# Sample-token values in column strips, state updates by quarters, shifted buffers and HGRN queries on VectorE in a two-layer hybrid decoder step

## The reference, cut to what matters

```python
for li in range(DEPTH):
    h = h + 0.5 * swiglu(rms_norm(h, ffn1_norm[li]), ffn1_w_gu[li], ffn1_w_down[li])
    u = rms_norm(h, mix_norm[li])
    m, s = gla_mixer(u, ...) if li % 2 == 0 else hgrn2_mixer(u, ...)
    h = h + m
    h = h + 0.5 * swiglu(rms_norm(h, ffn2_norm[li]), ffn2_w_gu[li], ffn2_w_down[li])
    gate = jax.nn.sigmoid(rms_norm(h, ple_norm[li]) @ ple_w_gate[li])
    h = h + gate * (p[li] @ ple_w_proj[li])
# in a mixer, for each head, with q, k, v and the gates g from u @ w_in:
#   S_t = diag(exp(g_t)) S_{t-1} + k_t^T v_t ;  o_t = scale * q_t S_t
# prompt: S_0 = 0; samples: S_0 is an input, and the state after 4 tokens is an output
```

## Time and profile before

| | |
|---|---|
| median of 3 runs | 2255.2 us (2254.94 to 2255.33) |
| the profiled execution | 2253.68 us, its span 2251.9 us |
| TensorE matmuls busy | 2235.1 us of the span, 99% |
| VectorE, ScalarE, GpSimd busy | 70%, 49%, 18% |
| DMA | 213.36 MB, mean 95 GB/s |
| granted TensorE clock | 0.997 of full |

### The profile page before, as it was taken

The page is one execution under the profiler, slowest core; times in us unless marked ns, Lnnn a source line. Parts: engine busy times, 40 slices in busy tenths (PEclk is TensorE's granted clock), DMA queues, the critical chain, the costliest instruction groups (busy, mean ns, idle before and its releaser), DMA issues.

```text
span 2251.9 us, 41846 instructions
## 1 busy us (share of the span) xinstructions
PE 2235.1 (99%) x17550; PEld 2185.3 (97%) x17550; DVE 1576.8 (70%) x2136; ACT 1093.0 (49%) x1581; POOL 395.0 (18%) x271
## 2 busy tenths in 40 slices
PE   9999999999999999999999999999999999999998
PEld 9999999988899999999999999998999999999998
DVE  7888833547578888635788884359678688886344
ACT  7555623353545555423555563255465555555234
POOL 3222101102121221000222210005022212220001
PEclk9999999999999999999999999999999999999999
DMA  5333423324242343233233333322342333333331
GB/s 135 111 97 95 115 85 83 88 73 127 66 134 78 94 112 101 86 106 86 66 109 99 94 99 96 107 66 67 94 118 76 99 94 94 101 106 102 87 95 50
DMA packets 387338, 213.36 MB, mean 95 GB/s; under 512 B 7007, under 2 KB 381438, under 8 KB 387150
## 3 DMA queue, kind: packets, MB, share of 16 engines
q1 hardware_dynamic: 386928, 210.59, 33.0%
q10 hardware_dynamic: 190, 0.05, 0.0%
q0 software_dynamic: 32, 0.03, 0.0%
HBM read 198.98 MB, written 11.67 MB: 94 GB/s over the span
## 4 chain that ended last, share of the span: by engine, by line
PE 95%; ACT 2%; DVE 2%; issue 1%; DMA 0%; SPq 0%; POOL 0%; ACTq 0%; DVEq 0%
PE ps L564 46%; PE ps L635 37%; PE ps L769 5%; PE ps L807 2%; PE ps L867 1%; PE ps L898 1%; PE ps L848 1%; PE ps L945 0%; PE ps L783 0%; DMA w_raw<-in_ffn_w_gu_dram 0%; DVE w_low L1754 0%; PE ps L914 0%; PE ps L881 0%; PE ps L930 0%; DVE u_low L1671 0%
## 5 line engine op out<-in xcount | busy, mean ns | idle before, releaser
L635 PE MATMUL ps<-u_diffs,w_high 128*128 128x272 f32 x2560 | 487.3, 288 | 2.2 <-DVE w_low L1754 1.7
L635 PEld LDWEIGHTS ps<-u_diffs,w_high 128*128 128x128 f32 x2560 | 401.6, 188 | 3.1 <-issue 3.0
L635 PE MATMUL ps<-u_diffs,w_low 128*128 128x272 f32 x1280 | 368.8, 288 | 0.0
L1658 DVE TENSOR_TENSOR w_low<-w_raw,w_high 128x1024 fp32r<-128x1024 f32 x205 | 263.0, 1301 | 91.7 <-ACT w_high L1114 91.4
L2337 POOL TENSOR_TENSOR hidden<-t_gate,t_up 128x544 f32<-128x544 f32 x84 | 191.3, 2278 | 715.8 <-ACT t_gate L1236 715.8
L564 PE MATMUL ps<-hid_high,w_high 128*128 128x272 f32 x1408 | 290.5, 287 | 0.0
L564 PE MATMUL ps<-hid_high,w_low 128*128 128x272 f32 x1408 | 289.5, 288 | 0.0
L564 PE MATMUL ps<-hid_low,w_high 128*128 128x272 f32 x1408 | 289.2, 287 | 0.0
L635 PE MATMUL ps<-u_high,w_low 128*128 128x272 f32 x960 | 278.3, 290 | 0.0
L635 PE MATMUL ps<-u_low,w_high 128*128 128x272 f32 x960 | 275.9, 287 | 0.0
L635 PE MATMUL ps<-u_high,w_high 128*128 128x272 f32 x960 | 275.3, 287 | 0.3 <-DVE w_low L1754 0.3
(11 more groups left out here) (282 smaller groups left out, 4211.4 us busy)
## 6 DMA issues: line engine op xcount, KB each, us to landing
w_raw<-in_ffn_w_gu_dram SPq DMA_DIRECT2D x176, 512.0 KB, 5.1
w_raw<-in_ffn_w_down_dram SPq DMA_DIRECT2D x64, 512.0 KB, 3.9
w_raw<-in_hgrn_w_in_dram SPq DMA_DIRECT2D x32, 512.0 KB, 4.2
w_raw<-in_gla_w_in_dram SPq DMA_DIRECT2D x25, 512.0 KB, 4.0
w_raw<-in_ffn_w_down_dram SPq DMA_DIRECT2D x32, 384.0 KB, 4.3
w_raw<-in_ple_w_gate_dram SPq DMA_DIRECT2D x16, 512.0 KB, 4.2
states_s<-in_state_gla_dram SPq DMA_DIRECT2D x8, 512.0 KB, 5.0
out_gla_s_dram<-states_s SPq DMA_DIRECT2D x8, 512.0 KB, 4.0
```

Of the source, the lines that this page charges most:

```text
L635: mm = pe.matmul(ps[:, bank, 0:HALF], half_slot(w, base, h)[:, k * P:(k + 1) * P], x(k), start=start and k == 0 and part == 0, stop=k == K ...
L1658: dve.tensor_tensor(WL[:, slot, :], RAW[:, slot, :], WH[:, slot, :].bitcast(F32), ALU.subtract)\
```

## The change

Values: the fifth token tile of `values` goes. In its place `sample_values` runs at the start of value units 1 and 3, each for two units: plain float32 matmuls with the 32 sample tokens stationary (`XS`, the sum of UH and UL, made once per layer by VectorE in `sample_tokens`) and 128 columns of `RAW` moving, one for each of four strips of 32 PSUM partitions, so that strip j holds the values of quarter j. ScalarE copies them with four smaller instructions. Since TensorE now reads `RAW`, the loads into slots of value units also wait for `vs_mm`.

States: `sequences` has two parts of four sequences, each with one matmul per sequence and quarter, in four row strips and banks 0, 1, 6 and 7. One transpose replaces two or four; VectorE multiplies its result with a larger `seqmask` into all eight `KM` at once, in place of ScalarE's two instructions. In HGRN the copy `KR` is dropped. The second part waits until VectorE has read the first. In `out_proj` VectorE adds the states in four portions behind the residual sums.

HGRN queries: VectorE scales them (`level_queries` between `level_keys` and `level_gates`), GpSimd only in GLA.

Norm by token: the fifth column of `rstd_tok` comes from four matmuls into the four strips.

Layout: 32 unused bytes before and the 64 bytes of `decay_chunk` in front of `u_high`, 32 unused and the 128 of the larger `seqmask` in front of `w_raw`, 96 unused behind `masks`. So u_high and u_low move by 96 bytes, the weights, the constants and `masks` by 256, the mixer and feed-forward region by 256.

```diff
-SEQ_PARTS = [(0, 1, 2), (3, 4, 5), (6, 7)]
-US_BANKS = [0, 6, 7]
+V_READ = {gr.v_unit + u: 2 * gr.gi + u // 2 + 1 for gr in GROUPS for u in range(4)}
+SEQ_PARTS = [(0, 1, 2, 3), (4, 5, 6, 7)]
+US_BANKS = [0, 1, 6, 7]
...
     H = sb("h_resid", [P, KT_D, T])
+    sb("pad_u", [P, 8])
+    DEC = sb("decay_chunk", [P, 4, NCH])
     UH = sb("u_high", [P, KT_D, T], F32R)
     UL = sb("u_low", [P, KT_D, T], F32R)
+    sb("pad_w", [P, 8])
+    seqmask = sb("seqmask", [P, N_SEQ, REP])
     RAW = sb("w_raw", [P, RING, UNIT])
...
-    seqmask = sb("seqmask", [P, 2, REP])
+    sb("pad_m", [P, 24])
...
-    DEC = sb("decay_chunk", [P, 4, NCH])
...
# SyncE, load_unit
                 sp.wait_ge(s["lo_made"], n - RING + 1)
+            if n - RING in V_READ:
+                sp.wait_ge(s["vs_mm"], V_READ[n - RING])
...
# TensorE, norm
-                for c in range(5):
-                    t0 = c * P if c < 4 else LASTTILE
-                    mm = pe.matmul(ps[:, 4, 300 + c:301 + c], ssq[:, t0:t0 + P], ones[:, 0:1], start=True, stop=True)
+                for c in range(4):
+                    pe.matmul(ps[:, 4, 300 + c:301 + c], ssq[:, c * P:(c + 1) * P], ones[:, 0:1], start=True, stop=True)
+                for j in range(REP):
+                    mm = pe.matmul(ps[32 * j:32 * j + 32, 4, 304:305], ssq[:, T_PROMPT:T], ones[:, 0:1], start=True, stop=True)
...
# TensorE, features and values
-                if gr.g == 1 and j < 3:
-                    sequences(GROUPS[gr.gi - 1], j)
+                if gr.g == 1 and j in (0, 2):
+                    sequences(GROUPS[gr.gi - 1], j // 2)
...
+            if u % 2:
+                sample_values(gr, u, n)
+            for c in range(4):
...
+        def sample_values(gr, u, n):
+
+            if u == 1:
+                pe.wait_ge(s["xs_made"], gr.layer + 1)
+                pe.wait_ge(s["diag_out"], gr.gi + 1)
+                if gr.has_r:
+                    pe.wait_ge(s["x_out"], 4)
+            for w in (u - 1, u):
+                slot = (n - u + w) % RING
+                for k in range(2):
+                    kk = 2 * w + k
+                    for j in range(4):
+                        mm = pe.matmul(ps[32 * j:32 * j + 32, V_BANKS[4], 0:P], XS[:, kk, :],
+                                       RAW[:, slot, k * 512 + j * P:k * 512 + (j + 1) * P],
+                                       start=(kk == 0), stop=(kk == KT_D - 1))
+            mm.then_inc(s["vs_mm"], 1)
...
# TensorE, mix and sequences
-            for h in range(NH):
-                mm = pe.transpose(ps[:, 0, h * P:(h + 1) * P], KR[:, h].rearrange("p j t -> p (j t)"), ident[:, :])
+            pe.transpose(ps[:, 0, 0:P], keys_s, ident[:, :]).then_inc(s["kds_turned"], 1)
...
-                pe.wait_ge(s["kmask_made"], 2 * gi + 2)
-                pe.wait_ge(s["var_ln"], 2 * gi + 1)
+                pe.wait_ge(s["kmask_made"], gi + 1)
+                pe.wait_ge(s["var_ln"], 2 * gi + 2)
             else:
-                pe.wait_ge(s["snew_made"], N_SEQ * gi + bs[-1] - 2)
...
+                pe.wait_ge(s["snew_made"], N_SEQ * gi + 4)
+            for b in bs:
+                for j in range(4):
+                    rows = slice(32 * j, 32 * j + 32)
+                    mm = pe.matmul(ps[:, US_BANKS[j], (b % 4) * P:(b % 4 + 1) * P], KM[rows, b, :], V[rows, 4, 0:P],
...
# ScalarE
-                    for j in range(REP):
-                        ins = act.activation(V[32 * j:32 * j + 32, c, :], ps[SROW:P, V_BANKS[c], :], ACT.Copy,
-                                             scale=rstdT[SROW:P, c:c + 1])
+                    act.wait_ge(s["vs_mm"], 2 * gr.gi + 2)
+                    act.activation(V[:, c, 0:P], ps[:, V_BANKS[c], 0:P], ACT.Copy, scale=rstdT[:, c:c + 1])
+                    for j in range(1, 4):
+                        rows = slice(32 * j, 32 * j + 32)
+                        ins = act.activation(V[0:T_SAMPLE, c, j * P:(j + 1) * P], ps[rows, V_BANKS[c], 0:P], ACT.Copy,
+                                             scale=rstdT[rows, c:c + 1])
...
-            for i in range(2):
-                act.activation(KM(i)[:, 0:NH * P], ps[:, 0, 0:NH * P], ACT.Copy, scale=seqmask[:, i, 0:1])\
-                   .then_inc(s["kmask_made"], 1)
...
# VectorE
             level_keys(gr, l)
+            if not gr.gla:
+                level_queries(gr, l)
             level_gates(gr, l)
...
+            for r in range(2):
+                ins = dve.tensor_tensor(compact(QTb[:, l % 2, :], gr, L, r), query_half(Q, gr, L, r),
+                                        compact(EQ, gr, L, r), ALU.mult)
+            ins.then_inc(s["qt_made"], 1)
...
+            dve.tensor_tensor(XS, UH[:, :, T_PROMPT:T].bitcast(F32), UL[:, :, T_PROMPT:T].bitcast(F32), ALU.add)\
+               .then_inc(s["xs_made"], 1)
...
+            dve.tensor_tensor(KM, ps[:, 0:1, 0:P].to_broadcast([P, N_SEQ, P]),
+                              seqmask[:, :, 0:1].to_broadcast([P, N_SEQ, P]), ALU.mult).then_inc(s["kmask_made"], 1)
...
# GpSimd
-            for l in range(LEVELS):
+            for l in range(LEVELS if gr.gla else 0):
```

More of the change, by code:

```diff
@@ L889, in mix @@
             pe.wait_ge(s["s_made"], 4 * gi + NCH - 1)
-            pe.wait_ge(s["ks_made"], gi + 1)
-            for h in range(NH):
-                mm = pe.transpose(ps[:, 0, h * P:(h + 1) * P], KR[:, h].rearrange("p j t -> p (j t)"), ident[:, :])
-            mm.then_inc(s["kds_turned"], 1)
+            if gr.gla:
+                pe.wait_ge(s["ks_made"], gi + 1)
+                keys_s = KR.rearrange("p h r t -> p (h r t)")
+            else:
+                pe.wait_ge(s["kdec_made"], N_KD[gi + 1])
+                keys_s = samples(K, gr)
+            pe.transpose(ps[:, 0, 0:P], keys_s, ident[:, :]).then_inc(s["kds_turned"], 1)
             def inter(j):
@@ L936, in sequences @@
             if part == 0:
-                pe.wait_ge(s["kmask_made"], 2 * gi + 2)
-                pe.wait_ge(s["var_ln"], 2 * gi + 1)
-            else:
-                pe.wait_ge(s["snew_made"], N_SEQ * gi + bs[-1] - 2)
-            for h in range(gr.NH):
-                hv = slice(h * gr.V, (h + 1) * gr.V)
-                for b in bs:
-                    rows = slice(32 * (b % 4), 32 * (b % 4) + 32)
-                    mm = pe.matmul(ps[:, US_BANKS[b % 3], hv], KM(b // 4)[rows, h * P:(h + 1) * P], V[rows, 4, hv],
+                pe.wait_ge(s["kmask_made"], gi + 1)
+                pe.wait_ge(s["var_ln"], 2 * gi + 2)
+            else:
+                pe.wait_ge(s["snew_made"], N_SEQ * gi + 4)
[3 more added lines that the diff above has]
+                    mm = pe.matmul(ps[:, US_BANKS[j], (b % 4) * P:(b % 4 + 1) * P], KM[rows, b, :], V[rows, 4, 0:P],
                                    start=True, stop=True)
@@ L976, in out_proj @@
             second_half(1)
-            sequences(last, 1)
             for m in range(2, KT_D):
@@ L987, in out_proj @@
                 if m == 2:
-                    sequences(last, 2)
+                    sequences(last, 1)
         def turn_chunk(out, rows, c):
@@ L1922, in features @@
                 n += 1
-                if gr.g == 1 and j < 3:
-                    sequences(GROUPS[gr.gi - 1], j)
+                if gr.g == 0 and j == 1:
+                    sample_tokens(gr)
+                if gr.g == 1 and j in (0, 2):
+                    sequences(GROUPS[gr.gi - 1], j // 2)
                 if gr.has_r and j >= gr.nfeat - 2:
@@ L1952, in features @@
             level_keys(gr, 6)
+            if not gr.gla:
+                level_queries(gr, 6)
             level_gates(gr, 6)
@@ L2168, in mix, with sequences @@
                 dve.tensor_tensor(og, og, ORS[:, j // gr.vt_per_head, :], ALU.mult).then_inc(s["og_made"], 1)
-        def sequences(gr, part):
-            dve.wait_ge(s["us_mm"], 3 * gr.gi + part + 1)
-            for b in SEQ_PARTS[part]:
+        def sequences(gr, part, i0=0, i1=4):
+            dve.wait_ge(s["us_mm"], 2 * gr.gi + part + 1)
+            for b in SEQ_PARTS[part][i0:i1]:
+                cols = slice((b % 4) * P, (b % 4 + 1) * P)
                 for h in range(gr.NH):
-                    hv = slice(h * gr.V, (h + 1) * gr.V)
-                    ins = dve.scalar_tensor_tensor(out=S0[:, b, hv], in0=S0[:, b, hv], scalar=DECS[:, h, b:b + 1],
-                                                   in1=ps[:, US_BANKS[b % 3], hv], op0=ALU.mult, op1=ALU.add)
+                    if gr.gla:
+                        st = S0[:, b, h * gr.V:(h + 1) * gr.V].rearrange("p (q v) -> p q v", q=2)
+                        new = ps[:, US_BANKS[2 * h]:US_BANKS[2 * h] + 2, cols]
+                    else:
+                        st = S0[:, b, h * gr.V:(h + 1) * gr.V]
+                        new = ps[:, US_BANKS[h], cols]
+                    ins = dve.scalar_tensor_tensor(out=st, in0=st, scalar=DECS[:, h, b:b + 1], in1=new,
+                                                   op0=ALU.mult, op1=ALU.add)
                 ins.then_inc(s["snew_made"], 1)
```

(10 more changed lines are left out.)

46 lines of the change are left out of this document (29 added, 17 removed).

## The result

The changed kernel takes 2236.5 us in the median of five runs (2235.13 to 2239.39), the kernel before 2255.2 (2254.94 to 2255.92) beside it: ratio 0.9922, 95% interval 0.9911 to 0.9933. The prediction was 2233.8 in a range of 2227 to 2243: the direction and the range hold, 2.7 us of the gain are missing.

What follows compares the result with a forecast made beforehand. TensorE's issue of matmuls was taken as the clock; -22.3 + 8.3 - 5.1 - 0.9 + 0.4 + 3.2 - 0.9 - 4.1 = -21.4 us from 2253.68 gave 2232.3, plus 1.5 for the median 2233.8, range 2227 to 2243.

Steps and rivals of the forecast that it cites:

- Values and strips: HGRN and GLA value units: fifth token tile removed, -22.3 us, float32 strip calls added, +8.3 us; net -14.0 us.
- rival 5: Sample values: the float32 strips run one after another, 21.5 us more over eight calls, 2255 us; chance 0.02.
- States, transposes, `norm`: TensorE: one state visit less per group -5.1 us, fewer key transposes -0.9, four one-column strips in `norm(by_token)` +0.4.
- VectorE holds up HGRN: HGRN value stage: TensorE waits for VectorE's mask, 1.8 us per group; +3.2 us together after the level 5 wait goes.
- Rival 2: HGRN value stage: VectorE does not hold it up, its lighter stretch starting early enough; -3.6 us, 2230.2 us; chance 0.10.
- rival 4: HGRN value stage: moving queries brings VectorE no relief, 71 us of work in a 64 us stage; 2251.6 us; chance 0.04.
- The load wait: Value units 0 and 1: loads held until `vs_mm` delay ScalarE's exponentials 1.5 us; costed at nothing, with 3 us margin.
- Rival 3: Value units: the wait of the loads reaches TensorE through ScalarE, 4 x 1.5 us, 2239.8 us; chance 0.08.
- The unused bytes: Gate tiles and Strassen-like loop: moved u_high and u_low shorten matmul intervals, -3.2 and -0.9 us, sum -4.1 (bounds -7.0, +7.0).
- the mixed loop: Strassen-like loop (L635) mixing u and u_diffs: moved addresses save 0.3 ns on 3 x 960 matmuls with u, -0.9 us.
- Rival 1: Layout: the unused bytes change nothing, the 0.9 ns being a difference between stages, not an experiment; 2237.9 us; chance 0.15.
- Rival 6: L564 and L635: 256 bytes before the weights slow some 14,900 float32r matmuls; at 2 ns each 2267.7 us; chance 0.04.

## Why the prediction was nearly right

- **Values and strips: right**, -14.0 forecast and -14.0 in the traces, 1.01 us a call with one end, which refutes rival 5, strips one after another. The shape measured at L881 in the trace of before carried over. The step as a whole was worth 10.0 us only, since the wait of the next point comes with it.
- **States, transposes, `norm`: right in kind**, 0.3 and 0.4 us off: a visit has eight passes whether three or four row strips run, 1.10 us as forecast, and four one-column strips cost no more than one.
- **VectorE holds up HGRN: right**, with the engine, the masks (of levels 0 and 1) and the levels as named, 1.4 us per group where I had 1.8. The size was off because TensorE reaches level 1 only 1.0 us before the mask and level 2 0.4 before it; with the first wait taken the second is short. Rival 2 is refuted by the wait's row, rival 4 by the 1.29 of L2031 and by the queries back on GpSimd. A new wait of 0.3 at L902 was not forecast.
- **The load wait: right at nothing**, but by 1.0 us and not by 3. Rival 3 has no row: ScalarE did stand still for the load, VectorE in the HGRN value stage did not.
- **The unused bytes: the step that failed.** I took 0.9 ns a matmul from the difference between the down stage and the gate tiles, and 0.3 for the mixed loop. A tile on u did gain (6.02 to 5.99 and, matmul by matmul, the intervals on u became those on hid_high), but over 3504 matmuls that is 1.0 us, not 3.2; the up stage lost 0.7 where I had a gain of 0.9. Without the bytes the time is 2236.4 instead of 2236.5. The premise that u takes over hid's interval by taking its place relative to the weights held for this one move and not in general: 32 bytes further hid changed and u did not. Rival 1, the bytes changing nothing, was right in its sum, its 2237.9 nearer to 2236.5 than my 2233.8, and so was its remark that a difference between stages is no experiment; single matmuls did change. The term is 3.8 us off. With the start and the states the misses of one sign are 4.7 us, those of the other 2.0; that only 2.7 are left is in part luck.
- **Rival 6**, 256 bytes before the weights making every matmul slower, did not happen: 134.47 against 134.40. But places 32 and 64 bytes away cost 7 to 11 us of work, so the interval does depend on where the weights lie, though a step of 256 did not change it.
- The profiled start was 0.6 us unlucky. I also had not reckoned with the time at half clock. It is the most likely cause of the 4.3 us between the fastest and the slowest of the five runs, whose mean clocks are 0.998 and 0.995.

By the Trainium skill (TensorE: Matmul & The Clock Gate, Step-by-step) the two read ports are independent, so the place of the weights should not matter; the runs say that it does, up to 1.7 ns a matmul, and the measurement decides. By the Trainium skill (TensorE: Matmul & The Clock Gate, Back-to-back issue gap) the formula that gave the prediction's 115.8 ns is that of a matmul by itself, not of a stream, so the 9 ns up to 124.5 do not contradict the page. By the Trainium skill (same page, Why this matters for your kernels) idle gaps between bursts of matmuls are what drops throughput in mid-kernel; here the granted clock fell to 0.50 in rows that show TensorE busy at 1.00, behind short matmuls.

## What to carry to other kernels

Price each part of a change from a piece of the same shape in the trace; such terms came out within 0.4 us. A difference in interval between two stages is not yet a gain to be had: move the address alone and sum the whole stage, since another loop may give it back. When TensorE's share shrinks in a stage where another engine is 97% busy, count only what that engine lets through, and look one engine further before reordering it.

## What the runs showed of the hardware

- The interval of 272-column float32r matmuls depends on where weights and moving operand lie: 124.4 ns in the down stage with the weights at the changed kernel's place or 128 bytes below, 125.6 with them 64 bytes below or above, 126.1 with 32 above. In both traces of the changed kernel it is the same to 0.1 ns.
- The up stage, which mixes two moving buffers, has its best places elsewhere (207.50 us where the down stage takes 135.61, 207.90 where it takes 134.40), so one layout does not serve both. Why is open.
- The granted clock fell to half for 3.4 us behind 24 plain float32 matmuls of 32 columns in a row, with TensorE never idle by the profile's rows, in one to three of four such places per execution, 24 of 48. With others between them it fell in none of the eight places of two traces.
- Column strips: a call of 32 records takes 1.01 us, and a visit of four row strips 1.10, as long as one of three.
